# A four-layer fp32 transformer kernel on one core: the mixers' end, the gate rows and the index projection rearranged

## The reference, cut to what matters

```python
# mLSTM: a decay-weighted linear attention in both directions
    h = (_mlstm_scan(q, k, v, ig_f, lf_f)
         + flip(_mlstm_scan(flip(q), flip(k), flip(v), flip(ig_b), flip(lf_b))))
    mu = jnp.mean(h, -1, keepdims=True)
    var = jnp.mean(jnp.square(h - mu), -1, keepdims=True)
    hn = (h - mu) * lax.rsqrt(var + 1e-5) * norm_g.reshape(MLSTM_HEADS, MLSTM_DH)
    y = jax.nn.sigmoid(o.reshape(shp).astype(F32)) * hn
...
# SSD: the same in another form, plus a skip, a gate by z and a norm over each group of 128
    y = (_ssd_scan(x, dt[:, :, 0], A[0], Bm, Cm)
         + flip(_ssd_scan(flip(x), flip(dt[:, :, 1]), A[1], flip(Bm), flip(Cm)))
         + x * d_skip.reshape(SSD_GROUPS, SSD_HPG)[..., None])
    y = y.reshape(Bsz, S, SSD_INNER) * jax.nn.silu(z.astype(F32))
    y = _rmsnorm(y.reshape(Bsz, S, SSD_GROUPS, SSD_INNER // SSD_GROUPS), ...)
```

## Time and profile before

| | |
|---|---|
| median of 3 runs | 2857.57 us (2857.41 to 2881.93) |
| the profiled execution | 2855.62 us |
| its span | 2853.8 us |
| DMA | 283.48 MB, mean 99 GB/s |
| DVE busy | 1473.9 us (52%) |
| ACT busy | 1204.7 us (42%) |
| POOL busy | 657.7 us (23%) |

### The profile page before, as it was taken

How to read it: one execution, slowest core, us unless ns; L and a number is a source line. 1 busy time by engine, 2 the same in 40 slices (tenths; PEclk the granted TensorE clock), 3 DMA queues, 4 the chain that set the end, 5 groups by cost and what they waited for, 6 DMA issues and landing times. The chain is left out here.

```text
span 2853.8 us, 33265 instructions
## 1 busy us (share of the span) xinstructions
PE 2514.1 (88%) x12712; PEld 2027.6 (71%) x12712; DVE 1473.9 (52%) x2350; ACT 1204.7 (42%) x2396; POOL 657.7 (23%) x348
## 2 busy tenths in 40 slices
PE   6999787966999688956998889999979989899998
PEld 6866676746866566745686768888776857788886
DVE  1755657853845657853598633232225985333222
ACT  2446626743436626733554622221136546222211
POOL 2401405753401405743350100000023501000000
PEclk9999888988999888986998999999979979999999
DMA  4200018953200019951220022222211301122221
GB/s 138 86 31 1 1 61 328 356 219 105 79 30 1 7 54 354 357 206 64 74 89 16 23 79 91 101 89 96 71 60 60 104 1 66 46 89 103 89 85 63
DMA packets 53214, 283.48 MB, mean 99 GB/s; under 512 B 12992, under 2 KB 12992, under 8 KB 26176
## 3 DMA queue, kind: packets, MB, share of 16 engines
q1 hardware_dynamic: 43840, 264.55, 25.8%
q0 software_dynamic: 9216, 16.80, 1.5%
HBM read 275.02 MB, written 23.07 MB: 104 GB/s over the span
## 5 line engine op out<-in xcount | busy, mean ns | idle before, releaser
L185 ACT ACTIVATE weights_hi<-weights_raw 128x2048 fp32r<-128x2048 f32 (+3 forms) x134 | 240.8, 1797 | 668.6 <-PE ps L208 603.0
L195 POOL TENSOR_TENSOR weights_lo<-weights_raw,weights_hi 128x2048 fp32r<-128x2048 f32 (+4 forms) x60 | 266.1, 4435 | 859.5 <-ACT weights_hi L185 817.8
L195 DVE TENSOR_TENSOR weights_lo<-weights_raw,weights_hi 128x2048 fp32r<-128x2048 f32 (+1 forms) x74 | 163.2, 2206 | 519.9 <-ACT weights_hi L185 519.9
L206 PE MATMUL ps<-y2t_hi,weights_hi 128*128 128x512 f32 x704 | 281.2, 399 | 10.2 <-PEq L1639 10.2
L207 PE MATMUL ps<-y2t_lo,weights_hi 128*128 128x512 f32 x704 | 279.8, 398 | 0.0
L208 PE MATMUL ps<-y2t_hi,weights_lo 128*128 128x512 f32 x704 | 278.1, 395 | 0.0
L206 PE MATMUL ps<-weights_hi,attn_ht_hi 128*128 128x512 f32 (+2 forms) x576 | 216.4, 376 | 4.7 <-PEq L229 4.7
L207 PE MATMUL ps<-weights_lo,attn_ht_hi 128*128 128x512 f32 (+2 forms) x576 | 213.7, 371 | 0.0
L208 PE MATMUL ps<-weights_hi,attn_ht_lo 128*128 128x512 f32 (+2 forms) x576 | 213.0, 370 | 0.0
L206 PEld LDWEIGHTS ps<-y2t_hi,weights_hi 128*128 128x128 f32 x704 | 133.2, 189 | 43.4 <-DVE weights_lo L195 10.9
L208 PEld LDWEIGHTS ps<-y2t_hi,weights_lo 128*128 128x128 f32 x704 | 133.0, 189 | 33.6
(11 more groups left out here) (475 smaller groups left out, 5738.0 us busy)
## 6 DMA issues: line engine op xcount, KB each, us to landing
weights_raw<-in_stream SPq DMA_DIRECT2D x110, 1024.0 KB, 4.8
weights_raw<-in_expert_gu SPq DMA_DIRECT2D x34, 1024.0 KB, 9.2
expert_raw<-in_expert_gu SPq DMA_DIRECT2D x30, 1024.0 KB, 9.3
expert_raw<-in_expert_down SPq DMA_DIRECT2D x18, 1024.0 KB, 8.0
weights_raw<-in_expert_down SPq DMA_DIRECT2D x14, 1024.0 KB, 8.1
weights_raw<-in_stream SPq DMA_DIRECT2D x12, 960.0 KB, 4.6
ln_more<-expert_rows SPq DMA_DIRECT2D x16, 512.0 KB, 7.4
weights_raw<-in_stream SPq DMA_DIRECT2D x8, 700.0 KB, 12.4
```

Of the source, the lines that this page charges most:

```text
L185: self.nc.scalar.activation(self.split_tiles(u)[0][:, 0:n], self.env.raw[:, u % self.RAW, 0:n], ACT.Copy).then_inc(self.hi_ready, 1)
L195: eng.tensor_tensor(lo[:, 0:n], self.env.raw[:, u % self.RAW, 0:n], hi[:, 0:n].bitcast(F32), ALU.subtract).then_inc(self.lo_ready, 1)
L206: nc.tensor.matmul(out, a[0], b[0], start=start, stop=False, **more)
```

## The change

Five edits, all in the two kinds of layers' first stages and in the decay stage.

1. The eight SSD units come before the eight mLSTM units.
2. `mixer_end_stage` goes; `MixerEnd` takes its place and puts its work between the units of the decay stage. The skip is part of the first SSD store; y is gated by z on DVE behind the store of unit 8 (units counted from 0), ACT squares it, one token tile behind the exponentials of each of units 11 to 14, DVE multiplies by the gain behind the store of unit 14, and each mLSTM head gets its mean, variance and gate (six instructions) when both its units are stored, that is behind the stores of units 9, 11, 13 and 15. Behind the last unit remain the last head's, two roots, one reciprocal, one product on DVE and eight scaled copies on ACT. POOL has none of it.
3. silu of z is computed in place on ACT in the first projection, sigmoid of o in place on ACT at the start of the MLA projection, and DVE multiplies it by the gain there.
4. The gate rows go back by 24 transposes of 8 or 16 partitions instead of 32 matmuls of 4 columns; m is no longer scanned as a row but added on the columns, so that DVE has six small instructions there instead of two.
5. The index key, weights and heads (584 columns) are projected as two jobs of 292 columns, each in two units of 1168 per partition. The rule for the rows of a unit is written anew; it gives other jobs what they had.

The rows spread by PE (L1124) are as before.

```diff
-        sums, c_, mx, m = ([scratch(2 + 2 * i + d)[0:16 if i == 0 else 8] for d in range(2)] for i in range(4))
+        sums, c_, mx = ([scratch(2 + 2 * i + d)[0:16 if i == 0 else 8] for d in range(2)] for i in range(3))
+        rows_back = ps[:, 5, 0:T * 64].rearrange("p (t c) -> p t c", t=T)
...
-                    for q, (src, rows, first) in enumerate(((c_, 8, 0), (mx, 8, 0), (m, 8, 0), (sums, 16, 8))):
+                    for src, rows, first in ((c_, 8, 0), (mx, 8, 16), (sums, 16, 32)):
                         for d in range(2):
-                            o = q * 8 + d * 4
-                            last = nc.tensor.matmul(ps[:, 5, t * 32 + o:t * 32 + o + 4],
-                                                    src[d][:, t * P:(t + 1) * P],
-                                                    ident[0:rows, first + d * 4:first + d * 4 + 4],
-                                                    start=True, stop=True)
+                            last = nc.tensor.transpose(rows_back[:, t, first + d * rows:first + (d + 1) * rows],
+                                                       src[d][:, t * P:(t + 1) * P], ident[0:rows, 0:rows])
...
+                    if (n, t) == (U + 1, 3):
+                        act.wait_ge(tile_stored, early * T)
+                        z = proj[:, :, SZ:SZ + SSD_H * SSD_P]
+                        nc.scalar.activation(z, z, ACT.Silu).then_inc(z_gated, 1)
...
-                    link(v.tensor_tensor_scan(mx[d][:, w], c_[d][:, w], c_[d][:, w], -3e38, ALU.max, ALU.bypass))
-                    last = v.tensor_tensor(m[d][:, :], mx[d][:, :], sums[d][0:8, :], ALU.add)
+                    last = v.tensor_tensor_scan(mx[d][:, w], c_[d][:, w], c_[d][:, w], -3e38, ALU.max, ALU.bypass)
...
-                src = ps[:, 5, 0:T * 32].rearrange("p (t c) -> p t c", t=T)
-                v.tensor_copy(cols[:, :, 0:24], src[:, :, 0:24])
-                v.tensor_scalar(cols[:, :, 24:32], src[:, :, 24:32], -1.0, None, ALU.mult)
+                for d in range(2):
+                    by_kind = rows_back[:, :, 0:32].rearrange("p t (q r) -> p t q r", q=2)[:, :, :, 12 * d:12 * d + 4]
+                    total = rows_back[:, :, 32 + 20 * d:36 + 20 * d]
+                    decay = rows_back[:, :, 40 + 20 * d:44 + 20 * d]
+                    v.tensor_copy(cols[:, :, 0:16].rearrange("p t (q r) -> p t q r", q=2)[:, :, :, 4 * d:4 * d + 4], by_kind)
+                    link(v.tensor_scalar(cols[:, :, 24 + 4 * d:28 + 4 * d], decay, -1.0, None, ALU.mult))
+                    v.tensor_tensor(cols[:, :, 16 + 4 * d:20 + 4 * d], cols[:, :, 8 + 4 * d:12 + 4 * d], total, ALU.add)
...
+            nc.scalar.activation(o_gate, o_gate, ACT.Sigmoid).then_inc(o_gated, 1)
...
+            dve.wait_ge(o_gated, 1)
+            vec.tensor_tensor(o_gate, o_gate, o_gain, ALU.mult)
...
                         dve.wait_ge(out_stored, j + 1)
+                    end.vector(dve, link, i - 1)
...
+                    end.scalar(act, i)
+                end.scalar(act, N)
...
+                if d == 0:
+                    x = proj[:, :, XBC + h * SSD_P:XBC + (h + 1) * SSD_P]
+                    return nc.vector.scalar_tensor_tensor(out=dst, in0=x, scalar=vec[:, V_SD + h:V_SD + h + 1], in1=out,
+                                                          op0=ALU.mult, op1=ALU.add)
...
+                if d == 0:
+                    return v.tensor_tensor(dst, out[:, :, 0:ML_D], per_tile(tmp[:, :], ML_D), ALU.mult)
...
+class MixerEnd:
+
+    GATE, SQUARES, GAIN, HEADS = 2 * SSD_H + 1, 2 * SSD_H + 3, 2 * SSD_H + 7, 2 * SSD_H + 2
+    LAST = 2 * SSD_H + 2 * ML_H
...
+    def head(self, link, h):
+
+        v = self.env.nc.vector
+        c = slice(h * ML_D, (h + 1) * ML_D)
+        hv, var = self.h_sum[:, :, c], self.stat[:, :, h]
+        link(v.reduce_sum(self.mean[:, :], hv, AX))
+        link(v.tensor_scalar(self.mean[:, :], self.mean[:, :], 1.0 / ML_D, None, ALU.mult))
+        link(v.tensor_tensor(hv, hv, per_tile(self.mean[:, :], ML_D), ALU.subtract))
+        link(v.tensor_tensor(self.sq[:, :, :], hv, hv, ALU.mult))
+        v.reduce_sum(var, self.sq[:, :, :], AX).then_inc(self.variances, 1)
+        link(v.tensor_tensor(hv, hv, self.proj[:, :, MO + h * ML_D:MO + (h + 1) * ML_D], ALU.mult))
+
+    def vector(self, dve, link, i):
+        v, y = self.env.nc.vector, self.y_ssd[:, :, :]
+        W = SSD_H * SSD_P
+        if i == self.GATE:
+            v.tensor_tensor(y, y, self.proj[:, :, SZ:SZ + W], ALU.mult).then_inc(self.gated, 1)
+        if i == self.GAIN:
+            dve.wait_ge(self.squared, T * SSD_G)
+            v.tensor_tensor(y, y, self.vec[:, V_SN:V_SN + W].unsqueeze(1).to_broadcast([P, T, W]), ALU.mult
+                            ).then_inc(self.times_gain, 1)
+        if i >= self.HEADS and (i - self.HEADS) % 2 == 0:
+            self.head(link, (i - self.HEADS) // 2)
+        if i == self.LAST:
+            dve.wait_ge(self.roots, 2)
+            v.reciprocal(self.stat[:, :, :], self.stat[:, :, :]).then_inc(self.inverse, 1)
+            dve.wait_ge(self.inverse, 1)
+            hf = self.h_sum.rearrange("p t (h c) -> p t h c", h=ML_H)
+            v.tensor_tensor(hf, hf, self.stat[:, :, 0:ML_H].unsqueeze(3).to_broadcast([P, T, ML_H, ML_D]), ALU.mult)
+
+    def scalar(self, act, i):
+        nc, G = self.env.nc, SSD_H * SSD_P // SSD_G
+        t = i - self.SQUARES
+        if t == 0:
+            act.wait_ge(self.gated, 1)
+        if 0 <= t < T:
+            if t:
+                act.wait_ge(self.squared, t * SSD_G)
+            for g in range(SSD_G):
+                nc.scalar.activation(self.ssd_sq[:, g, :], self.y_ssd[:, t, g * G:(g + 1) * G], ACT.Square,
+                                     accum_out=self.stat[:, t, ML_H + g:ML_H + g + 1]).then_inc(self.squared, 1)
+        if i == self.LAST:
+            act.wait_ge(self.squared, T * SSD_G)
+            ssd, heads = self.stat[:, :, ML_H:], self.stat[:, :, 0:ML_H]
+            nc.scalar.activation(ssd, ssd, ACT.Sqrt, scale=1.0 / G, bias=self.env.eps6).then_inc(self.roots, 1)
+            act.wait_ge(self.variances, ML_H)
+            nc.scalar.activation(heads, heads, ACT.Sqrt, scale=1.0 / ML_D, bias=self.env.eps5).then_inc(self.roots, 1)
+            act.wait_ge(self.times_gain, 1)
+            act.wait_ge(self.inverse, 1)
+            for t in range(T):
+                for g in range(SSD_G):
+                    y = self.y_ssd[:, t, g * G:(g + 1) * G]
+                    nc.scalar.activation(y, y, ACT.Copy, scale=self.stat[:, t, ML_H + g:ML_H + g + 1]).then_inc(self.scaled, 1)
...
-    for c, w, heads in ((B_IK, B_IW + IDX_H - B_IK, None), (B_IQ, BANK, None), (B_MQ, BANK, (0, (0, 1))),
+    index_half = (IN2 - B_IQ) // 2
+    for c, w, heads in ((B_IQ, index_half, None), (B_IQ + index_half, index_half, None), (B_MQ, BANK, (0, (0, 1))),
                         (B_DQ, BANK, (1, (0, 0))), (B_DK, BANK, (1, (1, 1))), (B_SQ, BANK, (2, (0, 1))),
                         (B_MV, 256, None), (B_SV, 256, None), (B_DV, BANK, None)):
-        rows = P * min(KD, WeightStream.UNIT // w)
+        rows = P * min(k for k in (1, 2, 4, KD) if 2 * k * w > WeightStream.UNIT or k == KD)
```

149 lines of the change are left out of this document (42 added, 107 removed).

## The result

The changed kernel takes 2778.94 us (median of 4 runs, 2775.24 to 2782.59) against 2857.49 us before: a ratio of 0.9707, 95% interval 0.9652 to 0.9761 (the ratio of the means, which takes in the one run before of 2881.93 us; the medians alone give 0.9725). The forecast was 2797, its range 2783 to 2815. The sign was right, the gain of 78.6 us is a third larger than the 58.7 us forecast, and it lies outside the range.

The account below looks back on a forecast made before the run. TensorE (PE), busy 2514 of 2853.8 us, was taken as the bound, through standing still and badly priced work. Gains of 13.6 + 14.6 + 30.5 = 58.7 us from 2855.6 gave 2797 us, range 2783 to 2815.

Parts of the forecast that it names:

- part 3: Index projection as two 292-column jobs: 28.0 us instead of 43.0 and 44.3, gaining 30.5 us over both layers.
- what it misses is covered by PE's wait for the rotation behind it: Next job's first 2048-column unit, ACT 1.9 and POOL 4.5 us, just fits in 6.5 us; any shortfall is hidden.
- a longer wait for the rotation: Sign of being wrong: the saved time comes back as a longer wait for DVE's rotation of the index heads.
- The 1.5 us at the half clock: Index jobs: 1.5 us added for 3 us at half speed, on top of 26.1 us for 192 matmuls.
- the other rule weighed there: Skill's rule for matmul spacing, columns over the clock: 72 + 512 cost what 2 x 292 do; part 3 gains only clock.
- The explanation by the clock: 72-column index job: granted clock 0.50 throughout, matmuls 0.21 us each; 350 columns regained full speed in 4 us.
- Part 2: Gate rows turned by 24 transposes at 2.8 us plus 0.7 us on DVE: gains 6.4 and 8.2, 14.6 us.
- Part 1: Mixers' end between the decay units: 18.9 us becomes 7.3, stage grows 4.8; 6.8 us gained per layer, 13.6 in all.
- the 4.8 us in the stage: Decay stage growth: 1.3 us for the first two heads, 3.5 for the third delaying the last unit's weighting.
- The heads did not serialise: Rival: DVE's heads collide with POOL's masks, each delaying PE fully; part 1 loses 3.6 us, time 2814; chance 0.13.
- 292 columns kept the clock: Rival: the 292-column index jobs don't earn the clock; part 3 is -6.9 instead of 30.5, time 2834; chance 0.09.
- The last rival: Clock falls in the decay stage from the first head on, 60 us in all, and part 3 fails; 2894 us; chance 0.03.

Follow-up runs that it names:

- key_copy_first: The kernel before with the two key copies made one instruction ahead of the scaling of the index weights; 2844.03 us in a single run.
- rotation_late: The changed kernel with one more DVE copy of 1152 elements ahead of the index rotation; 2796.35 us in a single run.
- heads_last: The changed kernel with all four mLSTM heads' ends behind the last unit instead of the first three between the units; 2785.09 us.
- order_only: The kernel before with only the SSD units moved ahead of the mLSTM units, mixers' end left behind them; 2860.79 us, ratio 1.0005.
- keys_last_job: The kernel before with its first two index jobs swapped, 512 columns first and 72 second; 2851.69 us, ratio 0.9975.

## Why the prediction was wrong in size and right in kind

**The failed step is in part 3.** It said of the next job's unit that "what it misses is covered by PE's wait for the rotation behind it". I had seen that wait and took it as a cover; it was a cost, 4.04 and 4.27 us and a slow stretch behind, that the change would take away. I had the port rule and applied it to the mixers' end, where nothing collided, and not here. I had also read it too narrowly, as a matter of instructions with two SBUF inputs: the one blocked at 338.73 in the earlier trace rows has a single input, and so have the key copies. That is 11.6 us of the 19 missing from the span, shown by key_copy_first and rotation_late. What I had named as a sign of being wrong, a longer wait for the rotation, was the opposite of what came. And that the race was won was luck: nothing in the change aimed at it, and two other splits of the same columns lost it.

**Part 3, the jobs.** 34.3 instead of 30.5 us. The price of a 292-column matmul (0.136) was right to 0.001 us. The 1.5 us at the half clock were there in some jobs and not in others (26.33 or 27.9 us in the profiles), and the 0.4 for the split came as 0.29 us. By the other rule weighed there, the spacing by columns over the clock, the jobs would have gained nothing but clock; with 72 columns and 248 both at 0.11 to 0.12 us the runs speak against it. The explanation by the clock was half right. "The granted clock was 0.50 during this whole job" and "the 72-column job never did" were wrong: it had the full clock at its start and lost it. So 72 columns have a price of their own, and they lose the clock on top.

**Part 2, the gate rows.** 17.1 instead of 14.6. The 2.8 us for 24 transposes came from transposes of 128 x 128; those of 8 and 16 partitions take 0.07 us each, 1.66 in all. That is 1.1 us per layer of the 1.25 missing. DVE's six instructions cost nearly what I gave them: 1.21 us from the last transpose to the next stage, where I had 0.7 on top of the 0.66 of before.

**Part 1, the mixers' end.** 10.6 instead of 13.6. What lies behind the last output, 7.3 us, was right. Of the 4.8 us in the stage, the 4.2 us wait came as 4.14, and the two heads as 1.0 instead of 1.3 (PE idle 0.37 us, the pair of units 10.51 us instead of 10.0). Missing was that PE, stopped for 4 us, runs its last output at the half clock, 2.1 us per layer. That is more than the 1.35 us by which the stage was mis-sized, and the row of the half-clock transposes at 351.39 in the earlier trace rows had it. Nor was the growth of that wait all the third head's: with the new order it is 1.77 us without any head (heads_last, order_only) where it was 0.50, a cost that the prediction had not given to edit 1.

**The rivals.** None came true. The heads did not serialise, 292 columns kept the clock or had it back some 3 us after losing it, and behind its first microseconds the decay stage kept it in the changed kernel up to the last wait. The last rival's mechanism exists, though, in the kernels with the old order. The range was too narrow below: its lower end took the known terms at their best, and no term stood for waits that the change would remove behind the places I looked at.

## What to carry to other kernels

A wait that the trace shows just behind an edit must be followed to its cause before it is counted as cover: here it hung on two instructions of 0.29 us against a 4.5 us one on a shared port, and 0.2 us decided over 5.8. Put the short instruction that others wait for first, and behind it what may be blocked. And work put into the holes of an engine goes where the engine that bounds the stage is busy with a long step of its own: a head's end cost PE 0.4 to 0.5 us ahead of the weighting that PE's next products needed, and nothing one unit later, beside the 3.7 us of these products.

## What the runs showed of the hardware

- A matmul of this kernel's split products costs 0.112 us at 72 columns (keys_last_job), 0.115 at 248, 0.135 at 292 and 0.155 at 336, all at the full clock: there is a floor. At the half clock 72 columns and 248 both cost 0.213 us and 292 cost 0.243, so at half the clock the floor is about twice as high.
- 72-column matmuls back to back lose the full clock without any stop of PE: 36 at 0.11 us, then 60 at 0.21 (keys_last_job, both layers).
- A DVE copy of 256 elements took 0.29 us free and 4.54 when it came 0.12 us behind POOL's split of 2048 columns (rotation_late).
- A stop of 4.14 us left PE at the half clock for a whole 20-matmul output (4.53 us instead of 2.44). One of 1.77 us did so for a part of it, which varies from profile to profile (3.02 us in one, 4.33 in another).
